# Layer 0's adaLN products set into the input projection by a table of tiles, in pieces twice as wide, and the first S5 parameter steps moved ahead of each mixer

## The reference

```python
cs = jax.nn.silu(c)
for l in range(DEPTH):
    mod = (cs @ w_ada[l] + b_ada[l]).reshape(B, 6, D)
    sh1, sc1, gt1, sh2, sc2, gt2 = [mod[:, i][:, None, :] for i in range(6)]
    h = rmsnorm(x, g_pre_mix[l]) * (1.0 + sc1) + sh1
    y = hybrid_mixer(h, ...)                  # h @ w_in, then mLSTM, S5 and NSA groups, then @ w_out
    x = x + gt1 * rmsnorm(y, g_post_mix[l])
    h = rmsnorm(x, g_pre_ffn[l]) * (1.0 + sc2) + sh2
    y = conv_ffn(h, ...)                      # h @ w_up, conv, gelu * u, @ w_down
    x = x + gt2 * rmsnorm(y, g_post_ffn[l])
```

```python
dt = jnp.exp(log_dt)[:, None]
mag = jnp.exp(lr * dt)
ar, ai = mag * jnp.cos(li * dt), mag * jnp.sin(li * dt)
den = lr * lr + li * li
zr, zi = ((ar - 1) * lr + ai * li) / den, (ai * lr - (ar - 1) * li) / den
```

## Time and profile before

| what | value |
|---|---|
| median of three runs | 2562.2 us (2557.14 to 2576.15) |
| the profiled execution, its own time | 2567.66 us |
| its span (first to last instruction) | 2565.9 us |
| TensorE / VectorE / ScalarE busy, of the span | 92% / 76% / 51% |
| mean granted clock of TensorE | 0.975 of full |

### The profile page before, as it was taken

One profiled execution on the slowest core, in us unless ns is written; L12 is line 12 of the kernel. 1 busy time (PEld: TensorE's weight loads), 2 busy tenths in 40 slices (PEclk: granted clock), 3 DMA queues, 4 the chain that ended last, 5 costly groups with the idle time before them and its releaser, 6 DMA issues.

```text
span 2565.9 us, 40251 instructions
## 1 busy us (share of the span) xinstructions
PE 2359.7 (92%) x13986; PEld 2070.4 (81%) x13986; DVE 1943.9 (76%) x2787; ACT 1304.5 (51%) x2085; POOL 261.6 (10%) x388
## 2 busy tenths in 40 slices
PE   0499889998999999999998999999799999999998
PEld 0499878866888888888878999886688888888886
DVE  7898888788999998866668966668898666665555
ACT  1465366546445455444448546564555545554444
POOL 0031311110111111100001211001010000000000
PEclk9799889999999999999999999999999999999999
DMA  9757777686999999868874665438597555556554
GB/s 405 308 193 273 281 275 242 233 338 213 333 347 339 333 341 339 323 221 273 273 246 165 206 238 201 133 132 338 208 346 272 190 189 188 188 188 190 195 190 154
DMA packets 187832, 644.09 MB, mean 251 GB/s; under 512 B 27248, under 2 KB 37488, under 8 KB 181568
## 3 DMA queue, kind: packets, MB, share of 16 engines
q1 hardware_dynamic: 120592, 457.00, 49.6%
q0 software_dynamic: 46512, 170.79, 19.4%
q10 hardware_dynamic: 20608, 14.72, 1.9%
HBM read 627.72 MB, written 14.71 MB: 250 GB/s over the span
## 4 chain that ended last, share of the span: by engine, by line
PE 75%; DVE 13%; DMA 5%; ACT 5%; issue 2%; ACTq 0%; SPq 0%; DVEq 0%; POOLq 0%
PE ps L1111 24%; PE ps L671 17%; PE ps L1112 12%; PE ps L654 11%; DVE w_lo L1610 4%; PE ps L991 3%; DVE ada_w L1616 2%; DVE mix L1610 2%; DMA ring<-ada_d 2%; ACT w_hi L1172 1%; DMA ring<-stream 1%; PE ps L639 1%; PE ps L790 1%; DVE mix L1616 1%; DMA s_own_w<-mix 1%
## 5 line engine op out<-in xcount | busy, mean ns | idle before, releaser
L1610 DVE TENSOR_TENSOR w_lo<-ring,w_hi 128x1024 fp32r<-128x1024 f32 x744 | 918.1, 1238 | 495.1 <-ACT w_hi L1172 491.7
L1172 ACT ACTIVATE w_hi<-ring 128x1024 fp32r<-128x1024 f32 x744 | 786.9, 1059 | 878.6 <-PE ps L1112 369.3
L1111 PE MATMUL ps<-hT,w_hi 128*128 128x512 f32 x2688 | 941.5, 396 | 0.3 <-DVE w_lo L1610 0.3
L1112 PE MATMUL ps<-hT,w_lo 128*128 128x256 f32 x2688 | 750.0, 279 | 0.0
L1111 PEld LDWEIGHTS ps<-hT,w_hi 128*128 128x128 f32 x2688 | 504.5, 188 | 122.4 <-DVE w_lo L1610 1.4
L1112 PEld LDWEIGHTS ps<-hT,w_lo 128*128 128x128 f32 x2688 | 506.3, 188 | 0.0
L654 PE MATMUL ps<-hT,w_hi 128*128 128x256 f32 x2496 | 475.1, 292 | 9.6 <-DVE w_lo L1610 9.3
L1616 DVE SCALAR_TENSOR_TENSOR ada_w<-ada_w,cs_row 128x1024 f32<-128x1024 f32 (+1 forms) x334 | 410.9, 1264 | 14.4 <-DMA ada_w<-ada_d 14.1
L654 PEld LDWEIGHTS ps<-hT,w_hi 128*128 128x128 f32 x2496 | 401.1, 197 | 18.2 <-issue 17.4
L654 PE MATMUL ps<-hT,w_lo 128*128 128x256 f32 x1248 | 359.1, 288 | 0.0
L654 PEld LDWEIGHTS ps<-hT,w_lo 128*128 128x128 f32 x1248 | 245.7, 197 | 0.0
(11 more groups left out here) (282 smaller groups left out, 2349.8 us busy)
## 6 DMA issues: line engine op xcount, KB each, us to landing
ring<-stream SPq DMA_DIRECT2D x760, 512.0 KB, 4.4
ada_w<-ada_d POOLq DMA_DIRECT2D x320, 512.0 KB, 6.4
ada_w<-ada_d SPq DMA_DIRECT2D x14, 1024.0 KB, 10.0
ring<-ada_d SPq DMA_DIRECT2D x12, 1024.0 KB, 10.3
mix<-ada_d SPq DMA_DIRECT2D x6, 1024.0 KB, 10.3
xs<-x SPq DMA_DIRECT2D x2, 2048.0 KB, 12.9
s_in_w<-mix ACTq DMA_DIRECT2D x8, 512.0 KB, 3.1
s_out_w<-mix ACTq DMA_DIRECT2D x16, 256.0 KB, 5.5
```

Source lines behind the costliest of these rows:

```text
L1111: pe.matmul(ps[:, bank, :], w_hi[:, s, ks], hT[:, k, :, :], start=k == 0, stop=False)
L1112: m = pe.matmul(ps[:, bank, SEQ:2 * SEQ], w_lo[:, s, ks], hT_hi[:, k, :], start=False, stop=k == KT - 1)
L1172: s.activation(w_hi[:, c % SPLIT, :], ring[:, at % RING, :], ACT.Copy).then_inc(hi_ready, 1)
L1610: return v.tensor_tensor(o, a, b, op)
```

## The change

**The modulation's place.** In layer 0's input projection a table `ADA_AT` now says how many pieces each turn does. **Its width.** `ada_group` does 128 x 2048 in one instruction over two `ada_w` slots, so 32 pieces take the place of 64 chunks, and needs no sum of halves; the same in up and down. (The output projection keeps `ada_chunk`.) POOL issues the first four loads at turn 0 instead of turn 13. **S5's first steps.** In layer 0 `s5_first`, `s5_second` and `s5_powers` run in the opening behind pieces 4, 8 and 12, with ACT's Exp and Sin for them ahead of its wait for `x`, and `s5_scaled` in turn 1. In layer 1 all four run in layer 0's down stage (behind its tiles 22, 26, 30 and 34), for which the parameter table is loaded at the start of that stage. **The rest.** `S5_B` is 4, 7, 10, 13; the first part of `aux` has 160 columns instead of 64; the last pieces of the output projection's modulation are 1 and 3 instead of 2 and 2.

```diff
-ADA_SLOT = 15
+ADA_AT = {2: 1, 3: 1, 12: 2, 15: 2, 16: 2, 17: 2, 18: 2, 22: 1, 23: 1, 25: 1, 26: 1, 27: 2, 28: 1, 30: 1, 31: 1, 32: 1,
+          33: 2, 34: 2, 35: 2, 36: 1, 37: 1, 38: 1, 39: 1}
 def ada_share(n, k):
-    return n * ACH * min(max(k + 1 - ADA_SLOT, 0), NT - ADA_SLOT) // (NT - ADA_SLOT)
+    return sum(m for t, m in ADA_AT.items() if t <= k) if n else 0
-GAINS = 4 * KT
+GAINS = A_OFF["f_conv_w"][0]
...
 # gpsimd
-                    if k == ADA_SLOT - 2 and N_IN[l]:
+                    if k == 0 and N_IN[l]:
                         for j in range(ASLOT):
                             ada_issue(j)
-                    for j in range(ada_share(N_IN[l], k - 1), ada_share(N_IN[l], k)):
+                    for j in range(2 * ada_share(N_IN[l], k - 1), 2 * ada_share(N_IN[l], k)):
...
+                if l < DEPTH - 1:
+                    gg_ready.wait(pool, l, 2)
+                    pool.dma_start(aux[:, :], aux_d[l + 1, :, :]).then_inc(aux_in, 16)
                 for a in range(N_DOWN[l]):
                     unit(U_DOWN[l] + a)
-                if l < DEPTH - 1:
-                    wait(w_used, l * NS + S_DOWN + 1)
-                    pool.dma_start(aux[:, :], aux_d[l + 1, :, :]).then_inc(aux_in, 16)
...
 # scalar, opening
+            s.wait_ge(gain_in, 16)
+            s5_step(0)
+            s5_angles(0)
             s.wait_ge(x_in, 16)
...
 # scalar, down
-                with s.Fori(0, 4) as i:
+                with s.Fori(0, 2) as i:
                     for k in range(10):
                         down(i, k)
+                for k in range(20):
+                    down(2 + k // 10, k % 10)
+                    if k == 0 and l < DEPTH - 1:
+                        s.wait_ge(aux_in, (l + 1) * 16 + 16)
+                        s5_step(l + 1)
+                    if k == 4 and l < DEPTH - 1:
+                        s5_angles(l + 1)
...
 # vector
+            def ada_group(u, g):
+                if g == 0:
+                    v.wait_ge(mod_ready, u)
+                at = 2 * g % ASLOT
+                for j in range(2):
+                    v.wait_ge(ada_full[at + j], (u - HEAD_UNITS) * (ACH // ASLOT * 16) + (16 * (2 * g // ASLOT) + 16))
+                w = ada_w[:, at:at + 2, :].rearrange("p a b -> p (a b)")
+                stt(w, w, 1.0, cs_row[:, :], ALU.mult, ALU.mult, ada_part[:, g, 0:1]).then_inc(ada_step, 2)
...
             for n in range(HEAD_UNITS * UG):
                 v.wait_ge(head_full[n % HEAD_SLOTS], n // HEAD_SLOTS * 16 + 16)
                 stt(head_slot(n), head_slot(n), 1.0, cs_row[:, :], ALU.mult, ALU.mult, head_sum[:, n:n + 1]).then_inc(ada_step, 2)
+                if n == HEAD_S5:
+                    s5_first(0)
+                if n == HEAD_S5 + 4:
+                    s5_second(0)
+                if n == HEAD_S5 + 8:
+                    s5_powers(0)
...
 # vector, input projection
-                    if k == 1:
-                        s5_first()
-                    if k == 3:
-                        s5_second()
-                    if k == 4:
-                        s5_powers()
-                    if k == 5:
-                        s5_scaled()
+                    if k == 1 and l == 0:
+                        v.wait_ge(aux_in, 16)
+                        s5_scaled(0, [pair(28 + 2 * i) for i in range(4)])
...
 # vector, down
+                        if l < DEPTH - 1:
+                            if (i, k) == (2, 2):
+                                s5_first(l + 1)
+                            if (i, k) == (2, 6):
+                                s5_second(l + 1)
+                            if (i, k) == (3, 0):
+                                s5_powers(l + 1)
+                            if (i, k) == (3, 4):
+                                s5_scaled(l + 1, [scratch[:, 512 * j:512 * j + 512] for j in range(4)])
...
-S5_B = (6, 9, 12, 15)
+S5_B = (4, 7, 10, 13)
```

175 lines of the change are left out of this document (92 added, 83 removed).

## The result

| kernel | median us | lowest to highest | runs |
|---|---|---|---|
| before | 2566.95 | 2557.14 to 2579.01 | 20 |
| after | 2578.34 | 2569.58 to 2585.48 | 20 |

The ratio is 1.003 (95% interval 1.0017 to 1.0043): the change costs some 8 us (the two medians are 11.4 us apart). 2528.0 was predicted, in 2512 to 2550. The profiled execution of after took 2576.03 us, its span is 2574.1, its mean granted clock 0.978.

The account below looks back on a forecast made before the run. TensorE bounds up and down; layer 0's input projection loses time to gaps where TensorE waits for VectorE. 2567.7 - 14.8 - 23.7 + 4.3 = 2533.5 us profiled, so a median of 2528.0, range 2512 to 2550.

Parts of the forecast that it names:

- Layer 0's own 34.2 us: Layer 0's input projection loses 34.2 us against layer 1's; 23.7 would go and 10.5 stay.
- the gaps of 8.2 and 3.4 us: TensorE's idle before `s5_in` and `s5_out` in layer 0's input projection, expected gone with less modulation in turns 19 to 26.
- The double turns: Turns with two pieces in layer 0's input projection: 4.5 us kept for 15 to 18, 3 for 27 and 33 to 35.
- A: Rival, chance 0.20: loads in tiles 15 to 18 and double turns starve the stream, `s5_own_w` lands late again; 2545 us.
- C: Rival, chance 0.04: bursts from POOL's queue at the opening and nine two-piece turns make it slower, costing 80 us; 2593 us.
- D: Rival, chance 0.07: gaps ending at VectorE stay because it waits for ACT and the ring; only S5's part gained; 2552 us.
- S5's 7.4 us in each layer: Both input projections: moving S5's first steps out removes a 4.7 us gap and its 2.7 us slow tile, 14.8 together.
- the two tiles by which the splits run ahead: Input projections: splits' lead of 11.5 us was to carry the first weight quarter, now in turns 4 and 5.
- Wider pieces in up: 0: Up stages: pieces of 2048 instead of two of 1024 cost nothing, since TensorE binds where most are.
- The down stage: 0: Layer 0's down: S5's added steps, 15 us of VectorE over fourteen tiles, cost 0, bounds 0 and 3.
- Opening's loads: 4.3: Opening: the modulation's early loads delay the stream's chunk before tile 0 by 4.3 us, bounds 0 and 5.1.
- S5 steps there, 0: Opening: S5's moved steps, 10.3 us of VectorE, fit into its waits for DMA; cost 0, up to 4.

Follow-up runs that it names:

- before_again: The kernel before, unchanged, profiled once more: 2565.12 us.
- narrow_late: The changed kernel with weight quarters at turns 6, 9, 12, 15 and modulation as before, S5's first steps still moved: 2562.71 us, ratio 0.9969 to before.
- table_narrow: narrow_late with layer 0's input-projection chunks in the changed table's turns, first loads at turn 0, each still 1024 wide: ratio 0.9981 to before.
- after_no_loads: The changed kernel with the modulation's products and loads in layer 0's input projection cut to 16 columns: ratio 0.9908 to before.

## Why the prediction was wrong

**Layer 0's own 34.2 us.** The step that failed is that less modulation beside the gaps of the earlier trace rows "takes away the gaps of 8.2 and 3.4 us" and most of the one before `weights_t`, priced at 23.7. Measured, against the mean of two profiles each (381.3 before, 382.6 after): nothing. Right was the gap before `s5_out`, which was VectorE's own work: 3.4 and 3.9 us, then 0.1 and none. But the gap before `s5_in` hangs on the DMA traffic, and the change loads as much as before: 6.9 and 5.7 us where before had 8.2 and 3.7. The gap before `weights_t` stayed (8.1 and 8.2 for 9.5 and 8.6), and 6.2 us before the transposes and 11.1 and 8.6 before L906 are new or grown. Emptying the products altogether, more than the change could take from VectorE, gave 4 to 11 us in the stage and 11 to 15 in the whole; 23.7 were put on moving them.

The double turns had been priced at 4.5 us (15 to 18) and 3 (27 and 33 to 35), the first from bytes against bandwidth. The bound was the time from a freed slot to the next landed load (6 to 14 us), of which a double turn has no spare. The waits for `ada_w` are the sign that the prediction gave for A and C. This is A's place, with another mechanism: the stream was not starved, the modulation was. D's wording (what ends a wait at VectorE isn't VectorE's own work) was nearer to it and had 0.07.

**The 34.2 was a draw besides.** Seven us of it, and 4.5 of the 8.2 us gap of the earlier trace rows, were that execution's: before_again has 377.8 us and 3.7 there. And the median of three that the forecast started from, 2562.2, is 2566.95 with twenty executions.

**S5's 7.4 us in each layer.** The mechanism was right and the place of the quarters wrong. With the quarters late layer 1 gains 4.5 us (348.9 to 344.4, 344.2 to 344.4 in four of the six kernels with quarters at 6, 9, 12, 15; the others 342.7 and 346.8), so 7.4 was too much there as well; with them early it gains nothing (348.8 to 353.6). The lower bound "0 if the quarter under POOL's products opens the same gap" was the answer. The failed step is that the two tiles by which the splits run ahead would carry the quarter: the wait is not for a split but for the quarter itself, whose transposes TensorE has in tiles 6 and 7.

**Wider pieces in up: 0.** Wrong by 3.2 us in up0 (492.5 for 489.3, two profiles each). With chunks three of the four slots load or stand ready while one is read, with a wide piece two. In up1 after has 491 us for 489.2, but narrow_late and table_narrow, without wide pieces, have 490.4 and 490.9: the width is not shown to cost there.

**The down stage: 0.** 253.4 for 251.2, 2.1 us; every kernel with S5's steps there has 252.1 or more, inside the bound of 3.

**Opening's loads: 4.3.** The mechanism held, the size didn't: tile 0 starts at 107.2 to 108.2 in the six profiles with the early loads and whole work, at 105.5 to 106.4 without (and at 106.05 in after_no_loads), so 1.7 us. The term that was too large is the stream's 0.128 MB per us while POOL's queue is full. That was read beside `aux`, with its large packets; beside the modulation's loads the stream moved 0.70 MB in 3.4 us, 0.206 per us. With equal shares the prediction's own figure was 2 us. It had put them down to sharing by bytes; the rows show turns by packets (190 and 187), of equal size. **S5 steps there, 0:** right.

The sum as measured from the two profiles each: opening +1.6, input 0 +1.3, output 0 and joint -1.8, up 0 +3.2, down 0 +2.1, layer 1's input +0.3, what follows it -0.5, up 1 +1.7 at equal pace (490.9 for 489.2): 7.9 us, where 0.003 of 2567 is 7.7. Rival C, slower, had its sign right and its place in the double turns too, but not its price: 76 us were put on what cost under 10.

## What to carry to other kernels

A gap that ends at an engine is not yet that engine's: cut the engine's work to nothing and leave its loads, then cut the loads, and the gap's rows say whose it is. Read the size from many executions, not from the one that was profiled. A piece twice as wide over the same slots leaves half as many pieces loading ahead, so it pays only where the next load is not waited for. A step that leaves a crowded place is worth its gap only if nothing else is put there.
